# Turned NSA queries, compressed scores in four pieces, up products by weight part, and a square root by ScalarE, in a hybrid attention and MLP block on one core

## What is computed

```python
def rmsnorm(x, w):
    xf = x.astype(jnp.float32)
    y = xf * lax.rsqrt(jnp.mean(xf * xf, axis=-1, keepdims=True) + EPS)
    return (y * w.astype(jnp.float32)).astype(x.dtype)
...
        s = jnp.einsum('bqghd,bngd->bghqn', qb, k_cmp).astype(jnp.float32) * scale
        dist = qpos[:, None] - cmp_end[None, :]
        s = s - slopes * dist.astype(jnp.float32)
        p_c = masked_softmax(s, dist >= 0)
        o_c = jnp.einsum('bghqn,bngd->bqghd', p_c.astype(v_cmp.dtype), v_cmp)
```

## Time and profile before

| | us |
|---|---|
| median of 3 runs (1102.70 to 1102.86) | 1102.71 |
| the profiled execution | 1102.36 |
| its span, first instruction to last | 1100.3 |
| PE busy | 1075.5 |
| DVE, ACT, POOL busy | 636.0, 496.2, 97.4 |

### The profile page before, as it was taken

One profiled execution on the slowest core, in us unless ns is written; L12 is line 12 of the kernel. 1 busy time (PEld: TensorE's weight loads), 2 busy tenths in 40 slices (PEclk: granted clock), 3 DMA queues, 4 the chain that ended last, 5 costly groups with the idle time before them and its releaser, 6 DMA issues.

```text
span 1100.3 us, 14215 instructions
## 1 busy us (share of the span) xinstructions
PE 1075.5 (98%) x5560; PEld 897.0 (82%) x5560; DVE 636.0 (58%) x782; ACT 496.2 (45%) x604; POOL 97.4 (9%) x159
## 2 busy tenths in 40 slices
PE   8999899899999999999999999999999999999996
PEld 7889787777777888888888888888888888888884
DVE  4555754777674555446545544555555654654565
ACT  4745544666663454334334433433433433443433
POOL 2136000331213000000000000000000000000003
PEclk9999999899999999999999999999999999999998
DMA  9576553142233556656566565565565556665552
GB/s 332 168 195 194 185 195 115 39 153 78 80 110 118 182 163 192 192 189 191 186 190 188 183 193 185 187 193 182 190 189 188 191 189 189 191 191 191 191 192 77
DMA packets 82993, 190.42 MB, mean 173 GB/s; under 512 B 8758, under 2 KB 21644, under 8 KB 82572
## 3 DMA queue, kind: packets, MB, share of 16 engines
q1 hardware_dynamic: 82524, 189.41, 54.1%
q10 hardware_dynamic: 432, 0.52, 0.2%
HBM read 187.82 MB, written 2.10 MB: 173 GB/s over the span
## 4 chain that ended last, share of the span: by engine, by line
PE 92%; DVE 4%; ACT 2%; issue 1%; DMA 0%; DVEq 0%; POOL 0%; ACTq 0%
PE ps L1566 21%; PE ps L1195 16%; PE ps L1196 15%; PE ps L1199 15%; PE ps L1568 11%; PE ps L1431 2%; PE ps L1405 1%; DVE w_lo L782 1%; PE ps L1260 1%; PE ps L1381 1%; PE ps L1432 1%; ACT w_hi L530 1%; PE ps L1384 1%; PE ps L1380 1%; PE ps L1385 1%
## 5 line engine op out<-in xcount | busy, mean ns | idle before, releaser
L782 DVE TENSOR_TENSOR w_lo<-raw,w_hi 128x2048 fp32r<-128x2048 f32 (+4 forms) x198 | 402.2, 2034 | 360.6 <-ACT w_hi L537 289.5
L537 ACT ACTIVATE w_hi<-raw 128x2048 fp32r<-128x2048 f32 x119 | 228.3, 1918 | 397.9 <-PE ps L1199 200.5
L1566 PE MATMUL ps<-xT,w_hi 128*128 128x512 f32 x1024 | 361.9, 398 | 1.3 <-DVE h_sb L966 1.0
L1568 PE MATMUL ps<-xT,w_lo 128*128 128x256 f32 x1024 | 287.4, 281 | 0.0
L1566 PEld LDWEIGHTS ps<-xT,w_hi 128*128 128x128 f32 x1024 | 192.3, 188 | 48.9 <-issue 1.3
L1568 PEld LDWEIGHTS ps<-xT,w_lo 128*128 128x128 f32 x1024 | 193.4, 189 | 0.5
L1196 PE MATMUL ps<-w_lo,hidT 128*128 128x512 f32 x448 | 174.5, 389 | 0.0
L1195 PE MATMUL ps<-w_hi,hidT 128*128 128x512 f32 x448 | 174.4, 389 | 0.0
L530 ACT ACTIVATE w_hi<-raw 128x1024 fp32r<-128x1024 f32 (+3 forms) x75 | 103.9, 1392 | 77.7 <-PE ps L1199 55.2
L1199 PE MATMUL ps<-w_hi,hidT 128*128 128x512 f32 x448 | 138.0, 389 | 0.0
L1195 PEld LDWEIGHTS ps<-w_hi,hidT 128*128 128x128 f32 x448 | 84.1, 188 | 17.7
(11 more groups left out here) (285 smaller groups left out, 1167.1 us busy)
## 6 DMA issues: line engine op xcount, KB each, us to landing
raw<-in_w_up SPq DMA_DIRECT2D x64, 1024.0 KB, 5.2
raw<-in_w_down SPq DMA_DIRECT2D x64, 1024.0 KB, 5.4
raw<-in_w_o SPq DMA_DIRECT2D x16, 1024.0 KB, 5.4
raw<-in_w_in SPq DMA_DIRECT2D x8, 1024.0 KB, 5.0
raw<-in_w_in SPq DMA_DIRECT2D x8, 816.0 KB, 4.4
raw<-in_w_in SPq DMA_DIRECT2D x6, 832.0 KB, 9.1
raw<-in_mla_w_uq SPq DMA_DIRECT2D x12, 256.0 KB, 4.2
raw<-in_mla_w_ukv SPq DMA_DIRECT2D x4, 512.0 KB, 5.5
```

Of the source, the lines that this page charges most:

```text
L537: act.activation(w_hi[:, j % SPLIT, :], raw[:, j % RAW, :], ACT.Copy).then_inc(hi_done, 1)
L782: return dve.tensor_tensor(dst, src, high.bitcast(F32), ALU.subtract)
L1566: pe.matmul(ps[:, b0 + f, :].rearrange("p (c t) -> p c t", c=2), w_hi[:, slot, w], xT[:, :, k0 + b, :], start=start and b == 0, stop=False)
L1568: m = pe.matmul(ps[:, b0 + f, 0:T], w_lo[:, slot, w], xT[:, 0, k0 + b, :], start=False, stop=stop and b == 3)
```

## The change

1. **Queries.** An `A_IN` chunk is now 8 blocks of 256 columns (rows of 1 KB in the load). The weights are stationary and the turned x moves as 256 columns: `q_products`, 48 matmuls a chunk. Queries come out turned; two chunks make a part, which is four heads. The root of the rows is needed along the columns: POOL spreads it, PE turns it by two transposes (`rows`), DVE copies it to `rrow`. DVE scales a part (`scale_queries`), ACT copies two high parts and DVE makes two low parts, at `("c", 0)` to `("c", 3)`: after chunk 25, in chunk 29, after step 14 and after step 19. Parts 2 and 3 are scaled at `out`, ahead of step 8. `turn_q` and `scores` are gone, and steps from the ninth on lie one quarter of a `w_o` chunk earlier.
2. **Compressed scores** in four pieces of 8 matmuls, at the `cmp` steps 12, 22, 32 and 42, which have no scores of their own, in the score banks 4 and 5 (`PIECES`, `TURN`). DVE adds biases, subtracts the smallest, ACT makes exponentials, and DVE weighs, piece by piece.
3. **Sum of squares** of the MLA output: at step 17, in a score bank.
4. **Up products**: for each f first the four of `w_hi`, then the four of `w_lo`.
5. **Last root**: ACT makes a square root, DVE its reciprocal and one Newton step. A square root of a constant ahead of the MLP makes ACT load its table there.

```diff
+SUM0 = NMLA + 9
+PIECES = {NMLA + 4 + 10 * p: p for p in range(4)}
+ROUND = [i for i, s in enumerate(STEPS) if s[0] != "cmp" or i in PIECES or i == SUM0]
+TURN = {i: r for r, i in enumerate(ROUND)}
...
-    PLAN += {CMP[1]: [("k", "rotary_k")], CMP[3]: [("k", "gelu")], A_IN[3]: [("k", "turn")]}.get(_c, [])
+    PLAN += {CMP[1]: [("k", "rotary_k"), ("k", "rows")], CMP[2]: [("c", 0)], CMP[3]: [("k", "gelu")], A_IN[3]: [("k", "turn")]}.get(_c, [])
...
-    PLAN += [("k", "project")] if _s == 0 else []
-    PLAN += [("s", _s), ("q", (_c, 2)), ("q", (_c, 3)), ("lo", (_c + 1, None))]
-    PLAN += [("k", "queries")] if _c == WO_M - 1 else []
-    PLAN += [("s", _s + 1)]
+    PLAN += [("k", "project"), ("c", 1)] if _s == 0 else []
+    PLAN += [("s", _s), ("q", (_c, 2)), ("q", (_c, 3)), ("lo", (_c + 1, None)), ("s", _s + 1)]
...
-PLAN += [("k", "turn_q"), ("s", NMLA), ("k", "scores"), ("s", NMLA + 1), ("k", "soft")]
-_s = NMLA + 2
+PLAN += [("k", "out"), ("s", NMLA)]
+_s = NMLA + 1
+ASIDE = {6: [("c", 2)], 11: [("c", 3)]}
...
             def score(i):
+                earlier = ROUND[TURN[i] - 2] if TURN.get(i, 0) >= 2 else None
+                if earlier in SOFT:
+                    pe.wait_ge(score_m, SOFT[earlier] + 1)
+                elif earlier in PIECES:
+                    pe.wait_ge(cs_in, PIECES[earlier] + 1)
+                elif earlier == SUM0:
+                    pe.wait_ge(ysum_ok, 1)
+                if i == SUM0:
+                    sum_over_features(0)
+                if i in PIECES:
+                    p = PIECES[i]
+                    pe.wait_ge(q_lo, 2 * p + 2)
+                    for c in (2 * p, 2 * p + 1):
+                        for t in range(TT):
+                            for e in range(2):
+                                o = 2 * (NC + 1) * (4 * (c % 2) + 2 * t + e)
+                                m = pe.matmul(ps[:, 4 + TURN[i] % 2, o:o + 2 * (NC + 1)], (q2a, q2b)[c // 4][:, e, c % 4, P * t:P * t + P],
+                                              kc2[:, c // 4, :, :].rearrange("p two n -> p (two n)"), start=True, stop=True)
+                    m.then_inc(cs_t, 1)
...
+            def q_products(c, only):
+
+                pe.wait_ge(lo_done, c + 1)
+                part, half, s = A_IN.index(c) // 2, A_IN.index(c) % 2, split_slot(c)
+                for quarter in range(4):
...
+                    for b in range(quarter // 2 * 4, quarter // 2 * 4 + 4):
+                        k = 8 * half + b
+                        w = slice(256 * b + P * f, 256 * b + P * f + P)
+                        pe.matmul(o, w_hi[:, s, w], xT[:, 0, k, :], start=k == 0 and f == 0, stop=False)
+                        m = pe.matmul(o, w_hi[:, s, w], xT[:, 1, k, :], start=False, stop=False)
...
+                        m = pe.matmul(o, w_lo[:, s, w], xT[:, 0, k, :], start=False, stop=k == KT - 1 and f == 1)
...
+            def scale_queries(part):
+                dve.wait_ge(w_used, A_IN[2 * part + 1] + 1)
...
+                dve.tensor_tensor(queries(part)[1], pairs(bank(part)), rrow[:, :].unsqueeze(1).broadcast_to((P, 2, T)), ALU.mult).then_inc(q_in, 1)
...
+                    both = ps[:, b0 + f, :].rearrange("p (c t) -> p c t", c=2)
                     for b in range(4):
-                        w = slice(512 * b + P * f, 512 * b + P * f + P)
-                        pe.matmul(ps[:, b0 + f, :].rearrange("p (c t) -> p c t", c=2), w_hi[:, slot, w], xT[:, :, k0 + b, :],
+                        pe.matmul(both, w_hi[:, slot, 512 * b + P * f:512 * b + P * f + P], xT[:, :, k0 + b, :],
                                   start=start and b == 0, stop=False)
-                        m = pe.matmul(ps[:, b0 + f, 0:T], w_lo[:, slot, w], xT[:, 0, k0 + b, :], start=False, stop=stop and b == 3)
+                    for b in range(4):
+                        m = pe.matmul(ps[:, b0 + f, 0:T], w_lo[:, slot, 512 * b + P * f:512 * b + P * f + P], xT[:, 0, k0 + b, :],
+                                      start=False, stop=stop and b == 3)
...
-                dve.tensor_scalar(minus, mean, -0.5, None, ALU.mult)
-                link(guess(y, mean))
-                for step in range(3):
-                    link(dve.scalar_tensor_tensor(out=w, in0=y, scalar=minus, in1=y, op0=ALU.mult, op1=ALU.mult))
-                    m = dve.scalar_tensor_tensor(out=y, in0=w, scalar=1.5, in1=y, op0=ALU.add, op1=ALU.mult)
-                    if step < 2:
-                        link(m)
-                m.then_inc(done, 1)
+                link(dve.tensor_scalar(minus, mean, -0.5, None, ALU.mult))
+                dve.wait_ge(sqrt_ok, t + 1)
+                link(dve.reciprocal(y, rm[:, t:t + 1]))
+                link(dve.scalar_tensor_tensor(out=w, in0=y, scalar=minus, in1=y, op0=ALU.mult, op1=ALU.mult))
+                dve.scalar_tensor_tensor(out=y, in0=w, scalar=1.5, in1=y, op0=ALU.add, op1=ALU.mult).then_inc(done, 1)
```

More of the change, by code:

```diff
@@ L100, in _step @@
         return [("k", "norm_n")] if s == len(STEPS) + LAG + 1 else []
-    return [("s", s)] + ([("k", "weigh")] if s == NMLA + 3 else [])
+    return [("s", s)] + ASIDE.get(s - NMLA, [])
 for _c in range(WO_M, WO_N + 4):
@@ L504, in _, with queries @@
             pool.tensor_scalar(third, third, rc[:, 0:1], None, ALU.mult).then_inc(last_w, 1)
+        def queries(part):
+            high = (q2a, q2b)[part // 2][:, :, 2 * (part % 2):2 * (part % 2) + 2, :]
+            return high, qfa[:, :, :] if part < 2 else qfb[:, part % 2, :, :]
         def sums_ready(eng, t, group, last):
@@ L646, in slot @@
                                    accum_out=den[:, n, 1:2]).then_inc(exp_ok, 1)
+                if i in PIECES:
+                    act.wait_ge(cs_sub, PIECES[i] + 1)
+                    part = pc[:, 2 * PIECES[i]:2 * PIECES[i] + 2, :, :, :].rearrange("p i t e n -> p (i t e n)")
+                    act.activation(part, part, ACT.Exp, scale=-1.0).then_inc(cs_exp, 1)
             for kind, i in PLAN:
@@ L668, in _ @@
                     act.activation(h1c[:, :, :], h1b[:, :, :], ACT.Tanh, scale=float(np.sqrt(2 / np.pi))).then_inc(g_th, 1)
[L669 to L681, removed]
+                elif kind == "c":
+                    act.wait_ge(q_in, i + 1)
+                    high, full = queries(i)
+                    for e in range(2):
+                        r = slice(64 * e, 64 * e + 64)
+                        act.activation(high[r, e, :, :], full[r, :, :], ACT.Copy).then_inc(q_hi, 1)
             def turned_hi(k):
@@ L751, in _, with square_root @@
                 square_sum(t, 0, 1024, 12 + 2 * t, t)
+            def square_root(t, last, before):
+                act.wait_ge(fsq, before)
+                act.wait_ge(rest_ok, t + 1)
+                act.activation(rm[:, t:t + 1], ssq[:, last:last + 1], ACT.Sqrt, scale=1.0 / D, bias=ssq[:, 12 + 2 * t:13 + 2 * t])\
+                    .then_inc(sqrt_ok, 1)
             act.wait_ge(last_in, 1)
             square_sum(0, 1024, D, 13, 2)
+            square_root(0, 13, 3)
             act.wait_ge(root0, 1)
@@ new lines, in _ @@
+                elif i == "rows":
+                    dve.wait_ge(rr_t, 1)
+                    dve.tensor_copy(rrow[:, :], bank(7, T)).then_inc(rr_ok, 1)
+                    dve.wait_ge(rr_ok, 1)
+                elif i == "out":
+                    for part in (2, 3):
+                        scale_queries(part)
+                elif kind == "c":
+                    if i < 2:
+                        scale_queries(i)
+                    high, full = queries(i)
+                    for e in range(2):
+                        r, other = slice(64 * e, 64 * e + 64), slice(64 - 64 * e, 128 - 64 * e)
+                        dve.wait_ge(q_hi, 2 * i + e + 1)
+                        low(high[other, e, :, :], full[r, :, :], high[r, e, :, :]).then_inc(q_lo, 1)
@@ L1443, in _ @@
                         pe.wait_ge(qp_out, 2)
-                    stream(c, of_x, 2 * j, LOW, j == 0, j == 7, None, quarter)
+                    q_products(c, quarter)
                 elif kind == "w":
```

179 lines of the change are left out of this document (96 added, 83 removed).

## The result

The changed kernel takes 1092.94 us (median of 4 runs, 1092.77 to 1093.46) against 1102.70 of the kernel before, measured beside it (4 runs, 1102.61 to 1102.86): a ratio of 0.9912, 95% interval 0.9899 to 0.9926. The forecast was 1089.9 in a range of 1086.5 to 1097.0: faster, as forecast, and 3.0 us less so. The profiled execution took 1092.80 us, 9.56 less than that of before.

A forecast was written before the change was run, and what follows sets the result against it. PE was taken as the bound, busy 1075.5 of 1100.3 us. Terms -8.5 - 0.3 + 2.5 + 0.2 - 5.0 - 1.7 = -12.8 gave 1089.6, plus 0.35 for the median 1089.9; range 1086.5 to 1097.0.

The forecast's parts named there:

- The bubble: PE's stretch from turning the queries to step 13, 25.68 us: 14.3 left, net -8.5 us after later pieces.
- The clock: Half-speed clock after the waits at the queries: gone if PE no longer stands still, 2.3 us of the 11.4 saved.
- Query chunks: Eight query chunks, each 48 matmuls of 256 columns instead of 24 of 512: +2.5 us, bounds 0 and +4.9.
- the transposes: Two PE transposes of `rows`, at 0.119 us each: +0.2 us.
- the later pieces: Three more pieces of compressed scores in later `cmp` steps: cost 2.85 us, already inside the net -8.5.
- the sum of squares: Moved from the place where PE waited 0.25 us for DVE to read it: -0.3 us, bounds 0 and -0.3.
- the waits that the rivals had: PE waiting on ACT's probability copies in steps, 1094.5 us, chance 0.10; or on DVE's query scaling, 1093.2, chance 0.06.
- The rows of 1 KB in the query weights' load: Query weights' load with shorter rows: nothing taken; upper end half a microsecond a chunk, 4 us.
- The tail: Last root at the kernel's end, five DVE instructions instead of ten, both passes together: -1.7 us, bounds -0.8 and -1.9.
- The up products: MLP loop's 896 pairs sorted by weight part lose most of 6.4 ns excess each: -5.0 us, bounds 0 and -5.7.
- the order of the up products moves nothing: Rival: the excess in the MLP loop's up products stays despite sorting, 1094.9 us; chance 0.25.
- four loads in a row are not hidden: Rival: loads beside 256-column up products set their pace at 189 ns, +56 us, some 1151; chance 0.05.

The follow-up runs named there:

- the two experiments on it: Up products alternating again in the changed kernel: 1094.26 us; up products sorted by weight part alone in the kernel before: 1101.05 us against 1102.57.

## Why the prediction was right, and where it was wrong

**The bubble.** Forecast: what is left of the stretch is 14.3 us. Measured: 15.76, with one quarter of `w_o` more, so 14.26. Its parts: a step without a wait 1.36 to 1.46 us instead of 1.36, a quarter 1.48 instead of 1.49, the piece 0.81 instead of 0.95, and the one late step 0.72 longer, where 0.7 was left for ACT. The 0.7 had been summed from idle times; one wait with 0.22 us of idle time cost as much, so this hit is partly luck. The clock stayed at 1.00, as forecast. The reason given, that PE no longer stands still, is borne out as far as a wait of 5.76 us at this place brings the clock down; that the shorter waits before had done so is not shown.

**Query chunks and the attention part as a whole.** Up to step 8 the changed kernel is 2.26 us late, 0.29 of it from ahead of the first query chunk: 1.97 where 2.5 for the chunks and 0.2 for the transposes were forecast. Behind step 13 it loses 3.36, where 2.85 for the later pieces less 0.3 for the sum of squares, 2.55, were forecast; the waits for DVE's adds, 1.0 us longer than before, were in no term. Up to the first up product the forecast is -8.5 - 0.3 + 2.5 + 0.2 = -6.1, and the traces show -5.8: two misses of 0.7 and 0.8 us cancel in it. Of the waits that the rivals had, PE has none for the query parts, and ACT was late in one step. The rows of 1 KB in the query weights' load, at which nothing was taken, left the wait ahead of the first query chunk as it was, 1.7 us; no run prices them apart.

**The tail.** Forecast -1.7, measured -1.9 in the trace and -1.8 alone.

**The up products are the step that failed**: -5.0 was forecast, -1.7 came. The pair went from 353.2 to 22.43 / 64 = 350.5 ns, not to the 347.6 on which the term stood. Two things in it were wrong. It took the excess to go with the seams or with the strict alternation, so that sorting by four leaves a quarter of it or nothing. The runs show the slowing behind a change spread over five wide products, so a group of four lies wholly within it, and only longer runs get past it. And it set nothing for the chunks ahead of the loop, where the alternating order had no excess to lose: sorted, they cost more, 0.33 us up to the second half round (with the order put back it is 463.22 - 372.08 = 91.14 us from the first up product to there, against 91.46 sorted). The prediction said that it did not know the cause of the excess; the value taken, 5.0, lay near the upper of its bounds of 0 and 5.7, and 1.7 came. Sixteen of a kind in a row bring pairs to 347.5 ns and give 3 of the 3.3 us that were missing.

The Trainium skill's gap of a matmul by its own columns ("TensorE: Matmul & The Clock Gate", section "Back-to-back issue gap": N/2.4 + 2.5 ns for a single one, an estimate of 215.8 for 512 columns) doesn't agree with this case: from one start to the next the same 512-column matmul took 226.7 ns in a pure stream and 224 to 241 behind narrow ones.

**The rivals.** That the order of the up products moves nothing is refuted by the two experiments on it. That four loads in a row are not hidden is refuted at four, 16 and 32 in a row: 113 to 120 ns each.

## What to carry to other kernels

Work that one engine does between two long streams of TensorE costs its idle time and, after a long wait, time at the lower clock (2.5 us behind one of 5.76 here); cut it into pieces and lay each where TensorE has other work. When a stream mixes matmuls of different width, try orders, and do not count changes alone: in this loop groups of four gained little over strict alternation and runs of 16 and 32 gained more, but ahead of the loop strict alternation was the fastest of all (5.55 us a chunk, against 5.61 in groups of four and 5.57 in runs of 16). An excess found in a trace is no gain until it is known what it hangs on: look at the intervals one by one, behind each kind of neighbour, before pricing an order that was not yet seen.

## What was not expected of the hardware

Behind 256-column matmuls, each with its own load, the next 512-column ones, in a run of 16, start 233, 236, 228, 233 and 231 ns apart instead of 226.7, alike within 1 ns in every round. In groups of four the first of these intervals stay so with the splits or the loads nearly taken away. Narrow matmuls with a load each run at 120 ns, the first behind a wide one at 113 or 114. The same strict alternation of the two ran at 347 ns a pair ahead of the loop and, after a single wait of 0.36 us, at 353 for the rest of it. The best kernel of these runs, at 1088.53 us, is the changed one with up products in runs of 16 and 32.
